# Convolution inputs and gates of the first mixer: from feature-major units to token-major seven-product passes

## The chip, the cores and the metric

The kernel runs on one core of one Trainium2 chip. The metric is the time of one execution on the device, in microseconds (us). PE is TensorE, ACT is ScalarE, DVE is VectorE, SP the queue that issues the DMAs.

## The reference

Two transformer-like blocks run over 256 tokens of width 2048, in float32. The change touches the first mixer of the first block:

```python
proj = h @ w_in        # q, k, v, g_out, gk_low, gate_b, gate_c, xc, merge_a, merge_b
o   = rmsnorm(gla_chunked(q, k, v, log_g))          # 4 heads of 512 value columns
y_a = o * silu(g_out)
y_b = gate_b * causal_depthwise_conv(gate_c * xc, conv_w)    # 3 taps
merged = sigmoid(merge_a) * y_a + sigmoid(merge_b) * y_b
out = merged @ w_out
```

The four projections `gate_c`, `xc`, `gate_b` and `merge_b` (2048 columns each, contraction over 2048) are what is recomputed in another form.

## The kernel before

Every float32 product is made of three products of rounded parts: a weight block W of 128x2048 is read from `raw` (four buffers, filled by SP), ACT rounds it into `w_hi` (L852, "high split"), DVE makes `w_lo` = W - `w_hi` (L1459, "low split"), and PE multiplies `w_hi` with both parts of x, then `w_lo` with the high part. `w_hi` and `w_lo` have two buffers each, so the high split of block n+2 waits until PE has ended the high part of block n, and its low split until PE has ended the low part of block n.

There are two ways to use a block. A *unit* (`unit`, L2540 and L2548) takes 128 output columns over the whole contraction and leaves them with features on partitions. A *pass* (`value_pass`, L2598 to L2623) takes 1024 output columns with tokens on partitions; for the first half of the contraction it makes seven block products where eight were needed (Strassen's scheme in a form due to Winograd: blocks of sums of weights and of x). A pass has 11 forms, each one block:

```python
GATE_1, GM_1, GM_5, GATE_2, GM_6, GM_3, GM_2, GM_7, UP_1, GM_4, UP_2 = range(GATE_FORMS)
```

Four of them (`GATE_1`, `GATE_2`, `UP_1`, `UP_2`) are long: 16 matmuls of `w_hi`, 8 of `w_lo`. The seven GM forms are short: 8 and 4. For four of the short ones DVE first makes a weight sum (`weight_sum`, 128x2048, L1604). ACT copies partial results out of PSUM in the middle of the pass (the state copies), and DVE adds the rest: two sums in the form `UP_1`, two at the start of the next pass.

Before, the stage order of the first mixer is: q and k as units; the values v in two passes; then the convolution stage, a loop over four heads; then `g_out` and `merge_a` in four passes, one for each head (the output passes); then `w_out`. One turn of the convolution loop is 16 units: for each of four tiles of 128 channels the units of `gate_c`, `xc`, `gate_b`, `merge_b`. Between them stand the steps of one head of the linear attention: PE makes the scores (L2874) ahead of unit 0 and the product with the values (L2882) ahead of unit 4; DVE masks the scores (L1684), makes their low part `sc_lo` (L1686) and the inputs of the next head (`stage`, L1556 to L1565); ACT squares the output (L963), takes a root (L966) and scales (L971). The convolution itself is done on DVE tile by tile (L1708 to L1728).

No scheduler is at work: each engine's program is written by hand in the order in which it runs, and semaphores join them. So an instruction that waits holds all that stand behind it on its engine.

## Time and profile before

| what | us |
|---|---|
| median of 3 runs | 2605.47 (2604.85 to 2606.33) |
| profiled execution: its own time | 2606.42 |
| profiled execution: its span | 2604.6 |
| PE busy | 2590.4 |
| DVE busy | 2083.6 |
| ACT busy | 1402.2 |
| conv stage on PE, first scores to first output pass | 190.76 to 564.20 |

The profile is of one execution. Busy time is the time in which an engine has at least one instruction under way. PE's rows overlap: a matmul of 128x512 is shown as some 390 ns long, while the next starts about 227 ns after it, so distances between starts, not durations, tell what PE's work takes.

### The profile page before, as it was taken

What the parts mean: (1) busy time and instruction counts of PE and PEld (TensorE: products, weight loads), DVE (VectorE), ACT (ScalarE), POOL (GpSimd) and SP (SyncE); (2) the same over time, 40 slices, a digit from 0 to 9 for tenths busy, and PEclk for the clock granted to TensorE, in tenths of its full rate; (3) what the DMA queues carried; (4) which work ended last, traced back from release to release, by engine and by line L of the source; (5) the groups of instructions that cost most, each with busy time, mean ns of one, the idle gap of its engine ahead of it and who ended that gap; (6) DMA issues with size and microseconds to landing.
All of it is one profiled execution on the core that took longest, in us unless ns stands there. A gap on an engine that the chain in (4) does not pass through costs nothing.

```text
span 2604.6 us, 34491 instructions
## 1 busy us (share of the span) xinstructions
PE 2590.4 (99%) x13138; PEld 2208.1 (85%) x13138; DVE 2083.6 (80%) x1902; ACT 1402.2 (54%) x1331; POOL 3.5 (0%) x8
## 2 busy tenths in 40 slices
PE   9999999999999999999999999999999999999998
PEld 8888888888888888888888888888888888888887
DVE  7886666679967999879998878897777787677888
ACT  6554444456756565546565556536554455444454
POOL 0000000000000000000000000000000000000000
PEclk9999999999999999999999999999999999999999
DMA  6464454546564646555655554534455545555554
GB/s 246 175 226 176 178 184 176 184 170 222 180 243 176 226 177 225 184 207 179 225 182 210 190 218 162 176 143 178 162 181 190 184 170 210 206 183 191 187 220 142
DMA packets 71892, 497.52 MB, mean 191 GB/s; under 512 B 8183, under 2 KB 9432, under 8 KB 12648
## 3 DMA queue, kind: packets, MB, share of 16 engines
q1 hardware_dynamic: 71784, 496.06, 52.6%
q8 instruction: 70, 1.15, 0.2%
q14 instruction: 38, 0.31, 0.0%
HBM read 493.93 MB, written 2.10 MB: 190 GB/s over the span
## 4 chain that ended last, share of the span: by engine, by line
PE 95%; DVE 2%; ACT 1%; DMA 1%; issue 0%; SPq 0%; DVEq 0%; ACTq 0%
PE acc L2540 27%; PE acc L2598 20%; PE acc L2548 14%; PE acc L2605 10%; PE acc L2623 6%; PE acc L2617 5%; PE acc L2619 5%; PE acc L2734 1%; DVE w_lo L1459 1%; ACT w_hi L852 1%; PE acc L2958 1%; DMA mask_s<-in_mask 1%; PE acc L2742 1%; PE aux L3040 1%; PE aux L3099 1%; DMA raw<-in_w_down 0%
## 5 line engine op out<-in xcount | busy, mean ns | idle before, releaser
L852 ACT ACTIVATE w_hi<-raw 128x2048 fp32r<-128x2048 f32 (+1 forms) x483 | 921.3, 1909 | 723.3 <-PE acc L2540 265.7
L1459 DVE TENSOR_TENSOR w_lo<-raw,w_hi 128x2048 fp32r<-128x2048 f32 (+1 forms) x483 | 1099.8, 2280 | 188.9 <-ACT w_hi L852 178.2
L2540 PE MATMUL acc<-xa,w_hi 128*128 128x512 f32 x3104 | 743.0, 391 | 0.0
L2540 PEld LDWEIGHTS acc<-xa,w_hi 128*128 128x128 f32 x3104 | 571.4, 188 | 112.3 <-issue 0.7
L2548 PEld LDWEIGHTS acc<-xa,w_lo 128*128 128x128 f32 x3104 | 397.9, 191 | 15.0
L2548 PE MATMUL acc<-xa,w_lo 128*128 128x256 f32 x3104 | 402.9, 283 | 0.0
L2598 PE MATMUL acc<-w_hi,xa 128*128 128x512 f32 x1152 | 273.2, 389 | 0.0
L2598 PEld LDWEIGHTS acc<-w_hi,xa 128*128 128x128 f32 x1152 | 215.9, 188 | 44.8
L2598 PE MATMUL acc<-w_hi,hid 128*128 128x512 f32 x768 | 183.3, 390 | 1.4 <-ACT w_hi L852 1.4
L1471 DVE TENSOR_TENSOR tmp<-acc,small 128x512 f32<-128x512 f32 x76 | 52.5, 691 | 150.7 <-ACT small L862 150.4
L2598 PEld LDWEIGHTS acc<-w_hi,hid 128*128 128x128 f32 x768 | 143.5, 188 | 32.0 <-ACT w_hi L852 2.2
L2605 PE MATMUL acc<-w_lo,xa 128*128 128x512 f32 x576 | 142.3, 389 | 0.0
L2605 PEld LDWEIGHTS acc<-w_lo,xa 128*128 128x128 f32 x576 | 108.1, 188 | 22.5
L852 ACT ACTIVATE w_hi<-w_sum 128x2048 fp32r<-128x2048 f32 x36 | 69.1, 1920 | 69.8 <-PE acc L2598 20.2
L1459 DVE TENSOR_TENSOR w_lo<-w_sum,w_hi 128x2048 fp32r<-128x2048 f32 x36 | 82.4, 2290 | 26.5 <-ACT w_hi L852 26.4
L1377 ACT ACTIVATE tmp<-tmp 128x256 f32<-128x256 f32 x44 | 18.4, 418 | 151.9 <-DVE tmp L2406 151.9
L2605 PE MATMUL acc<-w_lo,hid 128*128 128x512 f32 x384 | 95.2, 389 | 0.0
L2605 PEld LDWEIGHTS acc<-w_lo,hid 128*128 128x128 f32 x384 | 72.0, 188 | 15.0
L2617 PE MATMUL acc<-w_hi,xa 128*128 128x512 f32 x192 | 74.8, 390 | 0.0
L2619 PE MATMUL acc<-w_hi,xa 128*128 128x512 f32 x192 | 74.7, 389 | 0.0
L2617 PE MATMUL acc<-w_hi,g_hi 128*128 128x512 f32 x160 | 63.1, 395 | 0.0
L2619 PE MATMUL acc<-w_hi,g_lo 128*128 128x512 f32 x160 | 62.3, 390 | 0.0
(423 smaller groups left out, 2954.5 us busy)
## 6 DMA issues: line engine op xcount, KB each, us to landing
raw<-in_w_in SPq DMA_DIRECT2D x158, 1024.0 KB, 4.8
raw<-in_w_gate_up SPq DMA_DIRECT2D x88, 1024.0 KB, 4.8
raw<-in_w_down SPq DMA_DIRECT2D x88, 1024.0 KB, 4.8
raw<-in_w_up SPq DMA_DIRECT2D x87, 1024.0 KB, 4.8
raw<-in_w_out SPq DMA_DIRECT2D x32, 1024.0 KB, 4.8
raw<-in_w_uq SPq DMA_DIRECT2D x3, 1024.0 KB, 4.9
h_tok<-in_x_tok SPq DMA_DIRECT2D x1, 2048.0 KB, 10.7
raw<-in_w_ukv SPq DMA_DIRECT2D x4, 512.0 KB, 3.2
```

What stands on the lines that cost most here:

```text
L852: act.activation(hi_part(u, run)[:, 0:kt * P], raw_of(u)[:, 0:kt * P], ACT.Copy).then_inc(hi_made, splits(u, run))
L1459: dve.tensor_tensor(lo_part(u, run)[:, 0:kt * P], raw_of(u)[:, 0:kt * P], hi_part(u, run)[:, 0:kt * P], ALU.subtract).then_inc(lo_made, sp ...
L1471: dve.tensor_tensor(tmp[:, 0:2], acc[:, b:b + 2, 0:S], small[:], ALU.add).then_inc(acc_free, 2)
L2540: last = pe.matmul(acc[:, bnk], w_hi[:, u % SPLIT, k * P:(k + 1) * P], x[:, k0 + k], start=first and k == 0, stop=False)
L2548: last = pe.matmul(acc[:, bnk, S:2 * S], w_lo[:, u % SPLIT, k * P:(k + 1) * P], x[:, k0 + k, 0:S], start=False, stop=final and k == kt - 1)
L2598: last = pe.matmul(acc[:, bank(t + c)], a, w, start=(first and k == 0 and half == 0), stop=False, skip_group_check=more)
L2605: last = pe.matmul(acc[:, bank(t + c)], x[:, k0 + k, c * P:(c + 1) * P], lo_part(u, 0)[:, k * 512:(k + 1) * 512], start=False, stop=(final ...
L2617: pe.matmul(acc[:, bank(t)], x_hi(k), w, start=(first and k == 0), stop=False, skip_group_check=more)
L2619: last = pe.matmul(acc[:, bank(t)], x_lo(k), w, start=False, stop=False, skip_group_check=more)
L2623: last = pe.matmul(acc[:, bank(t)], x_hi(k), w_lo[:, u % SPLIT, k * 512:(k + 1) * 512], start=False, stop=(final and k == 3), skip_group_c ...
L2734: last = pe.matmul(acc[:, bank(tiles[c])], x[:, tile, half * S + c * P:half * S + (c + 1) * P], w_hi[:, u % SPLIT, k * 512:(k + 1) * 512], ...
L2742: last = pe.matmul(acc[:, bank(tiles[c])], x[:, tile, c * P:(c + 1) * P], w_lo[:, u % SPLIT, k * 512:(k + 1) * 512], start=False, stop=fin ...
```

## The change

The 64 units of the convolution stage become 8 passes (11 blocks each, 88 in all), two for each head: the first computes `gate_c` and `xc`, the second `merge_b` and `gate_b`. The results now have tokens on partitions and stand in `halves`. DVE multiplies the two of a pass with each other and with the row scale; PE transposes the product (8 transposes, `turn_product`) behind the form `GM_1` of the next pass; ACT makes the middle tap and DVE the two outer taps from the transposed tiles; the gate product is transposed too and multiplied in by `gated_conv_out`. The head's steps are put into the first pass of each pair: PE's scores behind `GATE_1`, the values behind `GM_2`. The high part of v is now made on ACT. The loop over heads is written out. In the second block's FFN, the first split of each first down pass is made a little earlier and one state copy is put behind a split. Here is the core of the diff:

On ACT:

```diff
+            def value_high(hd):
+                act.wait_ge(acc_free, T_V + 4 * (hd // 2) + 8)
+                act.activation(v_hi[:], v_tok[:, hd], ACT.Copy).then_inc(o_parts_made, 1)
+            def middle_taps(hd):
+                for t in range(4):
+                    i = 4 * hd + t
+                    act.activation(yb[:, i], aux[:, t // 2, t % 2 * S:(t % 2 + 1) * S], ACT.Copy,
+                                   scale=column("conv_w", i + 2 * DT)).then_inc(conv_mid, 1)
+            def conv_gate(hd):
+                for c in range(2):
+                    act.wait_ge(acc_free, T_CONV + 8 * hd + 4 + c + 5)
+                    act.activation(halves[:, c], halves[:, c], ACT.Sigmoid, scale=rstd_t[:, c:c + 1]).then_inc(gate_out, 2)
...
+            for k, u in enumerate(CONV_STARTS):
+                hd, second = k // 2, k % 2
+                for form in range(GATE_FORMS):
+                    if form == GM_7:
+                        conv_state(k, GM_7, 3, 1)
+                    split(u + form + 2)
+                    if form == GM_1 and not second:
+                        value_high(hd)
+                    if form == GM_5:
+                        if k:
+                            act.wait_ge(turned, k + 1)
+                        conv_state(k, GM_1, 3, 0)
+                    if form == GATE_2:
+                        conv_state(k, GM_5, 2, 3)
+                    if form == GM_6:
+                        conv_state(k, GM_6, 3, 2)
+                        if second:
+                            middle_taps(hd)
+                        else:
+                            act.wait_ge(masked, hd + 1)
+                            act.activation(sc_hi[:], sc[:], ACT.Copy).then_inc(sc_hi_made, 1)
+                    if form == GM_2:
+                        prepare(ACT.Sigmoid if second else ACT.Sqrt)
+                    if form == GM_7 and not second:
+                        act.wait_ge(o_made, hd + 1)
+                        for c in range(2):
+                            act.activation(o_n[:, c], aux[:, c], ACT.Square, accum_out=o_sum[:, c:c + 1]).then_inc(o_squared, 1)
+                    if form == UP_1 and not second:
+                        act.wait_ge(var_made, hd + 2)
+                        act.activation(o_var[:], o_var[:], ACT.Sqrt).then_inc(std_made, 1)
+                    if form == GM_4 and not second:
+                        act.wait_ge(o_scale, hd + 1)
+                        for c in range(2):
+                            act.activation(v_tok[:, hd, c], aux[:, c], ACT.Copy, scale=o_rstd[:, c:c + 1]).then_inc(o_read, 1)
+                if second:
+                    conv_gate(hd)
```

On DVE:

```diff
+            def conv_sum(k, form, tile, n, state):
+                u = CONV_STARTS[k]
+                dve.wait_ge(lo_used, u + form + 1)
+                dve.wait_ge(snapped, sums_before(u) + state)
+                dve.tensor_tensor(halves[:, n], halves[:, n], acc[:, bank(T_CONV + 4 * k + tile)], ALU.add).then_inc(acc_free, 1)
...
+            def conv_product(k):
+                conv_sum(k, UP_2, 2, 2, 3)
+                conv_sum(k, UP_2, 3, 3, 2)
+                dve.wait_ge(acc_free, T_CONV + 4 * k + 8)
+                if k % 2:
+                    dve.wait_ge(gate_out, 2 * k + 4)
+                for c in range(2):
+                    dve.scalar_tensor_tensor(halves[:, c], halves[:, 2 + c], (rstd_t if k % 2 else rstd_2)[:, c:c + 1], halves[:, c],
+                                             ALU.mult, ALU.mult).then_inc(gate_in, 1)
...
+            def outer_taps(hd):
+                for back in (1, 2):
+                    for t in range(4):
+                        i = 4 * hd + t
+                        if back == 1:
+                            dve.wait_ge(conv_mid, i + 1)
+                        elif t == 0:
+                            step.wait()
+                        tail = yb[:, i, back:S]
+                        step(dve.scalar_tensor_tensor(tail, aux[:, t // 2, t % 2 * S:(t % 2 + 1) * S - back],
+                                                      column("conv_w", i + (2 - back) * DT), tail, ALU.mult, ALU.add))
+            def gated_conv_out(hd):
+                dve.wait_ge(turned, 2 * hd + 3)
+                step.wait()
+                y = yb[:, 4 * hd:4 * hd + 4]
+                dve.tensor_tensor(y, y, aux[:, 2:4].rearrange("p b (a s) -> p (b a) s", s=S), ALU.mult).then_inc(op_f32, 4)
...
+            for k, u in enumerate(CONV_STARTS):
+                hd, second = k // 2, k % 2
+                if k:
+                    conv_product(k - 1)
+                for form in range(GATE_FORMS):
+                    split(u + form + 2)
+                    if form == GATE_1:
+                        weight_sum(u, 2)
+                    if form == GM_5:
+                        weight_sum(u, 3)
+                        if not second:
+                            value_low(hd)
+                    if form == GATE_2 and not second:
+                        dve.wait_ge(scores_made, hd + 1)
+                        dve.tensor_tensor(sc[:], aux[:, 0, 0:3 * P], mask_s[:], ALU.mult).then_inc(masked, 1)
+                    if form == GM_3:
+                        weight_sum(u, 4)
+                        if not second:
+                            dve.wait_ge(sc_hi_made, hd + 1)
+                            dve.tensor_tensor(sc_lo[:], sc[:], sc_hi[:], ALU.subtract).then_inc(o_parts_made, 1)
+                    if form == GM_7:
+                        if second:
+                            outer_taps(hd)
+                        else:
+                            if hd:
+                                gated_conv_out(hd - 1)
+                            if hd + 1 < HEADS:
+                                stage(hd + 1)
+                    if form == UP_1:
+                        conv_sum(k, GM_2, 0, 0, 1)
+                        conv_sum(k, GM_4, 1, 1, 4)
+                        if not second:
+                            dve.wait_ge(o_squared, 2 * hd + 2)
+                            dve.tensor_scalar(o_var[:], o_sum[:], 1.0 / DV, EPS, ALU.mult, ALU.add).then_inc(var_made, 1)
+                    if form == GM_4:
+                        if not second:
+                            dve.wait_ge(std_made, hd + 2)
+                            dve.reciprocal(o_rstd[:], o_var[:]).then_inc(o_scale, 1)
+                        weight_sum(u + GATE_FORMS, 1)
+            conv_product(2 * HEADS - 1)
```

On PE (`scores` and `head_values` are the matmuls of L2874 and L2882 behind their new waits):

```diff
                 by_tokens(u + GATE_1, b_11, xa, 8, 4, True, False)
+                if scores:
+                    scores()
...
                 product(u + GM_2, b_11, *block_of(xa, 4, 0), final=True)
+                if values:
+                    values()
...
+            def scores(hd):
+                pe.wait_ge(staged, hd + 1)
+                pe.wait_ge(gate_in, 4 * hd + 2)
...
+            def head_values(hd):
+                pe.wait_ge(o_parts_made, 3 * hd + 3)
...
+            def turn_product(k):
+                pe.wait_ge(gate_in, 2 * k + 4)
+                pe.wait_ge(*((op_f32, 4 * (k // 2)) if k % 2 else (o_read, k + 2)))
+                for m in range(4):
+                    for c in range(2):
+                        at_ = m % 2 * S + c * P
+                        last = pe.transpose(aux[:, k % 2 * 2 + m // 2, at_:at_ + P], halves[:, c, m * P:(m + 1) * P], ident[:])
+                last.then_inc(turned, 1)
...
+            for k, u in enumerate(CONV_STARTS):
+                value_pass(u, T_CONV + 4 * k, (lambda: turn_product(k - 1)) if k else None,
+                           *(((lambda: scores(k // 2)), (lambda: head_values(k // 2))) if k % 2 == 0 else ()))
```

In the second FFN, on ACT and DVE (the down passes' first splits):

```diff
+                        if g == 0 and form == M_7:
+                            first_out(u, t, 3, M_7, 2 * p, 1)
+                        if p or form != PLAIN_1:
+                            split(u + form + 2)
                         if g == 0 and form == M_6:
...
+                        if last and p:
+                            weight_sum(u0 + 2 * GT, 1)
+                            split(u0 + 2 * GT + M_1)
```

The order of the instructions on two engines shows where the head's steps now stand. First DVE, in the middle of the first pass of head 1 (L1459 before and L1492 now are the low split, L1604 and L1636 the weight sum). Before, one turn of the loop has, between two of the head's splits:

```order
L1714 SCALAR_TENSOR_TENSOR qkv<-tmp,vec,qkv 128x254
L1683 REGISTER_ALU
L1684 TENSOR_TENSOR sc<-aux,mask_s 128x384
L1686 TENSOR_TENSOR sc_lo<-sc,sc_hi 128x384
L1456 REGISTER_ALU
L1459 TENSOR_TENSOR w_lo<-raw,w_hi 128x2048
```

And now:

```order
L1764 TENSOR_TENSOR sc<-aux,mask_s 128x384
L1492 TENSOR_TENSOR w_lo<-raw,w_hi 128x2048 x2
L1636 TENSOR_TENSOR raw<-raw,v_sum 128x2048
L1769 TENSOR_TENSOR sc_lo<-sc,sc_hi 128x384
L1492 TENSOR_TENSOR w_lo<-raw,w_hi 128x2048 x2
L1748 TENSOR_TENSOR qkv<-qkv,aux 128x1024
```

The low part of the scores has moved from right behind the mask to behind two splits and a weight sum.

Second ACT, around the root of the head's variance (L852 before and L854 now are the high split, L963/L1006 the squares, L971/L1013 the scaled copies). Before:

```order
L862 ACTIVATE small<-acc 128x512
L965 REGISTER_ALU
L966 ACT_TABLE_LOAD
L966 ACTIVATE o_var<-o_var 128x2
L849 REGISTER_ALU
L852 ACTIVATE w_hi<-raw 128x2048
```

And now, from the squares on:

```order
L854 ACTIVATE w_hi<-raw 128x2048
L1006 ACTIVATE o_n,o_sum<-aux 128x512 x2
L854 ACTIVATE w_hi<-raw 128x2048
L1009 ACTIVATE o_var<-o_var 128x2
L854 ACTIVATE w_hi<-raw 128x2048
L1013 ACTIVATE v_tok<-aux,o_rstd 128x512 x2
L854 ACTIVATE w_hi<-raw 128x2048
L854 ACTIVATE w_hi<-v_sum 128x2048
L854 ACTIVATE w_hi<-raw 128x2048
```

The root and the copies now stand directly between the high splits of the last forms of the pass and of the first forms of the next one.

## Rows read from the trace of the kernel before

**Rows 1.** Page, parts 1 and 4: busy time by engine, chain that ended last.
```profile
PE 2590.4 (99%) x13138; PEld 2208.1 (85%) x13138; DVE 2083.6 (80%) x1902; ACT 1402.2 (54%) x1331; POOL 3.5 (0%) x8
...
PE 95%; DVE 2%; ACT 1%; DMA 1%; issue 0%; SPq 0%; DVEq 0%; ACTq 0%
```

**Rows 2.** Waits of PE over the span (us in total, times, longest).
```profile
PE acc L2598 <- ACT w_hi L852: 1.4, 2, 0.8
```

**Rows 3.** Windows, us, then busy PE, PEld, DVE, ACT, POOL; PEclk: three stretches.
```profile
149.96:190.76 40.80, 40.80 (x181) 33.78 (x180) 34.53 (x19) 23.41 (x16) 0.00 (x0) 1.00 0.56 205
...
286.30:379.60 93.30, 93.30 (x543) 82.58 (x542) 62.54 (x72) 42.28 (x38) 0.00 (x0) 1.00 0.50 180
...
605.02:646.73 41.71, 41.71 (x189) 34.61 (x188) 39.54 (x27) 29.42 (x25) 0.00 (x0) 1.00 0.54 199
```

**Rows 4.** Timeline of PE: two units of the convolution's input, by rows of weights.
```profile
222.88 3.82 PE L2540 MATMUL acc<-xa,w_hi 128*128 128x512 f32 x16
...
228.45 3.82 PE L2540 MATMUL acc<-xa,w_hi 128*128 128x512 f32 x16
```

**Rows 5.** Timeline of PE in the third output pass.
```profile
673.94 1.07 PE L2623 MATMUL acc<-w_lo,v_hi 128*128 128x512 f32 x4
674.85 3.79 PE L2598 MATMUL acc<-w_hi,xa 128*128 128x512 f32 x16
...
696.64 1.04 PE L2901 MATMUL aux<-ident,v_tok 128*128 128x128 f32 x8
```

**Rows 6.** Timeline of ACT in the same pass.
```profile
667.86 0.58 ACT L997 ACTIVATE m_tok<-acc 128x512 f32<-128x512 f32 x1
668.75 1.92 ACT L852 ACTIVATE w_hi<-raw 128x2048 fp32r<-128x2048 f32 x1 [0.32 <-PE acc L2619]
...
675.54 1.91 ACT L852 ACTIVATE w_hi<-raw 128x2048 fp32r<-128x2048 f32 x1
```

**Rows 7.** Timeline of DVE in the same pass.
```profile
670.71 2.29 DVE L1459 TENSOR_TENSOR w_lo<-raw,w_hi 128x2048 fp32r<-128x2048 f32 x1 [0.43 <-ACT w_hi L852]
672.92 2.28 DVE L1604 TENSOR_TENSOR raw<-raw,out_sum_w 128x2048 f32<-128x2048 f32 x1
675.12 4.66 DVE L1459 TENSOR_TENSOR w_lo<-raw,w_hi 128x2048 fp32r<-128x2048 f32 x2
679.69 1.65 DVE L1742 SCALAR_TENSOR_TENSOR qkv<-aux,vec,qkv 128x256 f32<-128x256 f32 x4
681.27 2.28 DVE L1459 TENSOR_TENSOR w_lo<-raw,w_hi 128x2048 fp32r<-128x2048 f32 x1
683.47 1.28 DVE L1756 TENSOR_TENSOR g_tok<-g_tok,acc 128x512 f32<-128x512 f32 x2
684.66 1.22 DVE L1749 TENSOR_TENSOR xb<-qkv,xb 128x1024 fp32r<-128x1024 f32 x1
```

**Rows 8.** Timelines of ACT and DVE: four scaled copies; two 512-column products.
```profile
770.36 1.55 ACT L1029 ACTIVATE xa<-aux,vec 128x256 fp32r<-128x256 f32 x4
...
152.56 1.40 DVE L1647 SCALAR_TENSOR_TENSOR v_tok<-acc,rstd_t,v_tok 128x512 f32<-128x512 f32 x2
```

**Rows 9.** Groups by line in the conv stage: the head's small operations.
```profile
L971 ACT ACTIVATE v_tok<-aux,o_rstd 128x512 f32 x8 | 5.0, 675 | 0.0
...
L1686 DVE TENSOR_TENSOR sc_lo<-sc,sc_hi 128x384 fp32r<-128x384 f32 x4 | 2.2, 558 | 2.4 <-ACT sc_hi L959 2.4
...
L966 ACT ACTIVATE o_var<-o_var 128x2 f32<-128x2 f32 x4 | 0.8, 204 | 0.0
```

**Rows 10.** Timeline of DVE: first of the nine of `stage`, and the split behind them.
```profile
235.96 0.16 DVE L1556 COPY dec<-e_b 128x8 f32 x1
...
239.03 2.29 DVE L1459 TENSOR_TENSOR w_lo<-raw,w_hi 128x2048 fp32r<-128x2048 f32 x1 [0.30 <-DVE q_far L1565]
```

**Rows 11.** Windows at the end of the program, columns as in rows 3.
```profile
2590.00:2597.00 7.00, 6.22 (x28) 4.81 (x26) 5.20 (x11) 1.04 (x4) 0.00 (x0) 1.00 0.33 112
2597.00:2600.00 3.00, 0.00 (x0) 0.00 (x0) 2.90 (x7) 0.99 (x3) 0.00 (x0) 0.85 0.20 77
```

More of the change, by code:

```diff
@@ L1377, in gated @@
                         act.activation(tmp[:, 2], tmp[:, 2], ACT.Gelu_apprx_tanh).then_inc(gate_out, 1)
[L1378 removed]
+                        if not (ahead == 2 and p == 0):
                             split(u + 4, run)
@@ L2391, in _, with gated @@
                 v0, g0 = V_FF2 + g * GT, G_FF2 + g * GT
-                def gated(run, pairs, ahead=0, between=None):
+                def gated(run, pairs, ahead=0, between=None, last=False):
                     for p in range(2):
```

211 lines of the change are left out of this document (62 added, 149 removed).

## The prediction

> **What bounds the kernel now.** I read the page first: PE is busy for 99% of the span and makes 95% of the chain that ended last [rows 1]. In the list of PE's waits the first entry is 1.4 us, in two waits of at most 0.8, at the start of the second FFN's down passes [rows 2]. So the kernel is PE's own work, back to back, and a change pays by what it takes off PE, less what it makes PE wait. The windows by stage then tell how near the others are: in a value pass DVE is busy for 34.5 of 40.8 us, in a head of the convolution stage for 62.5 of 93.3, in an output pass, which also has transposes and merges, for 39.5 of 41.7 [rows 3]. The new passes are of that last kind and carry more, so the timelines of PE, ACT and DVE in one output pass are what the rest is worked out from [rows 5 to 7].
>
> **PE's own work.** A unit takes 5.57 us from start to start [rows 4], eight of them 44.5; a pass for the same 1024 columns takes 40.8 [rows 3]. Eight passes save 8 x 3.73 = 29.8 us. Each pass's product is turned by 8 transposes: the output pass with transposes is 41.71, the one without 40.80, so 0.91 each, 8 x 0.91 = 7.3 us back. Scores and values are the same matmuls as before. PE's work alone: -22.5 us. In the down passes the earlier split can give back up to the 1.4 us of [rows 2]; I take -1.4, the other end is 0.
>
> DVE's work grows too: 11 low splits and 4 weight sums a pass, 2.2 us each from start to start [rows 7], are 33 us; four sums 2.4, two products 1.4 [rows 8]. With the head's steps the first pass of a pair comes to some 43 of PE's 45.9 us, the second to some 40 of 41.7. On the average this fits. But a pass has fixed meeting points, and the sum of busy times does not show them. I walk through them in order of time, against T, PE's end of the form `GM_7` (674.85 in [rows 5]). From T, PE has `UP_1` 5.44, `GM_4` 2.72, `UP_2` 5.44 and the next `GATE_1` 5.44: it wants `GATE_1` at T+13.6 and `GM_1` at T+19.1 (the transposes behind `GM_1` start at 696.64, less 2.72).
>
> **Wait 1, values for the low scores, four times.** In the output pass PE starts the low part of `GM_7` at 673.94, so `GM_7` itself began, and `GM_2` ended, at 672.13. DVE's weight sum 4 began at 672.92 and its next instruction at 675.12, 3.0 us behind `GM_2` [rows 5, 7]. It can't be earlier: its split of `GM_7` waits for ACT's high split, which ACT starts when PE has ended the high part of `GM_3` (668.75, idle 0.32 before it [rows 6]). In the first pass of a head `sc_lo` stands behind this weight sum, 0.56 us [rows 9], and PE's values stand ahead of `GM_7`. With a hop of 0.1 between engines and 0.1 for the high part of the scores on ACT, PE waits 3.8 us: 15.2 us. That DVE doesn't take `sc_lo` sooner is in its order: the pair of splits at 675.12 starts right behind the weight sum [rows 7]. The Trainium skill (TensorE: Matmul & The Clock Gate, Architectural detail) says that ACT and DVE are strict FIFO; this trace agrees. Were it otherwise, `sc_lo` could go ahead of the weight sum, the wait would be 1.6 us, and the sum below would be 8.8 us lower.
>
> **Wait 2, `GATE_1` of the second pass, heads 1 and 2.** DVE has ended the splits behind T at T+4.84 (679.69). Now follow `gated_conv_out` 1.1 (1024 columns, half of a split's 2.2), `stage` 3.07 [rows 10], a split 2.2, two sums 1.2 (busy 1.28, [rows 7]), the variance 0.2: T+12.6. ACT's root, 0.20 [rows 9], stands ahead of the high split of the next `GATE_1`, 1.92: ready at T+14.9, against 13.6. 1.3 us for heads 1 and 2, 0.15 for head 0 (no product of a head before it), none for head 3 (no `stage`): 2.8 us.
>
> **Wait 3, `GM_1` of the second pass, four times.** From that high split on: low split 2.3, reciprocal 0.2, ACT's two scaled copies 1.3 [rows 9], the high split of `GM_1` 1.9, its low split 2.2, the two sums 1.2 that free PE's last bank, hops: 9.2 us, while PE has 5.44 of `GATE_1`. 3.8 us for heads 0 to 2. For head 3 DVE is 3.1 us earlier and PE waits from T+19.1 to T+21.3: 2.2. Together 13.6 us.
>
> **Wait 4, scores for the product, three times.** In the second pass ACT makes four middle taps (1.55 us, [rows 8]) between its state copy at 667.86 and the high split at 668.75. That split, and DVE's chain behind it, come 1.1 us later; the low part of `GM_7` waits 0.2 (four times, 0.8 us), and DVE ends the two splits at T+5.8. Then eight taps 3.35 (two groups like L1742's, 1.58 each, and a drain), split 2.2, sums 1.2, split, weight sum, split 6.6, sums 1.2: T+20.3; the two products 1.4 and hops: T+21.9. PE's scores stand at T+19.1 and wait for it: 2.8 us for heads 1 to 3, 8.4 us. Ahead of the first output pass `GM_1` waits for the sums alone: 1.3.
>
> **The sum.** -29.8 + 7.3 + 15.2 + 2.8 + 13.6 + 0.8 + 8.4 + 1.3 - 1.4 = +18.2 us. On the profiled execution's own 2606.4 that is 2624.6; the median of the runs is 0.9 below that execution, so **2623.7 us**, slower by 0.7%. What I cost at nothing: the DMAs (as many blocks of the same size as before, and the same freeing order as in the output passes, where PE doesn't wait for them), the high part of v on ACT (half of a high split's 1.92 us, in a form in which ACT has time: it is busy for 29 of 41.7 us [rows 3]), and the written-out loop. Were this cover gone, each late load would be one more wait of PE's. Bounds: the gate product and the taps, which read PSUM, may take what a 512-column pair takes in [rows 8] (0.3 us more each); each of the 18 waits may be 0.3 us off either way. That gives 2617 to 2631 for this case.
>
> **Rivals.** (a) *PE never waits.* DVE's total fits, and the sum of PE's work alone decides: 2606.4 - 22.5 - 1.4, median 2581.6, faster. It needs DVE to run ahead of PE, which the double buffers of `w_hi` and `w_lo` forbid: in [rows 7] DVE itself idles 0.43 us for ACT's high split. Chance 0.04. (b) *Only wait 1 is real.* At the pass ends DVE catches up, because taps, `stage` and the small steps overlap better than start-to-start distances say. The point is the sums' end, T+19.1; if they are there, waits 2 to 4 are nothing: 2606.4 - 22.5 - 1.4 + 15.2, median 2596.8, faster by 0.3%. For it: an output pass with 39.5 us of DVE's work doesn't wait at all. Against it: that pass has no `stage`, and no root between two high splits. Chance 0.09. (c) *Half of waits 2 to 4*, median 2610, chance 0.05. (d) *The clock falls in the long waits.* PE's last matmul ends at 2596.2 (6.22 us busy of the first 7), and in the next window the granted clock is 0.85 as a mean, so it fell from the upper level (2.4 GHz) to the lower (1.2 GHz) about 3 us after PE went idle [rows 11]. Waits 1 and 3 are 3.8 us, seven in all. If each is followed by as long a stretch at half speed, each costs 1.9 us more, 13 us: median 2637. The page named above (Part 1) holds that an idle array goes to the lower clock and that sustained work brings it back; the rows show the first. How soon it comes back no row shows; the waits of [rows 2] are too short to tell. Chance 0.12.
>
> **How the numbers follow.** Forecast 0.70, (a) 0.04, (b) 0.09, (c) 0.05, (d) 0.12. The range runs from 2609, which leaves out (a), (b) and a part of (c), to 2635, which leaves out the far half of (d). A measurement of this kernel tells a change of 0.2%, 5.2 us, from none. Faster by more than that: (a) and (b), 0.12. Within it, up to 2610.7: half of (c) and a little of the forecast, 0.06. Slower: 0.82.
>
> **What would show it.** In the changed profile PE should wait, in the list of waits, for `sc_lo` four times by 3.8 us, for the sums of `halves` in the second passes by 3.8, for the products ahead of the scores by 2.8, and for ACT's high split once or twice by 1.3. Passes should last about 50, 46, 52, 47, 52, 47, 52 and 44 us, the stage from the first scores on some 20 us longer than the 373 of before. If the first pass of a head lasts 46 us, wait 1 is wrong; if the second lasts 42, waits 2 and 3 are. A granted clock below 1.00 inside the stage speaks for (d).

## The result and the profile after

| what | before | after |
|---|---|---|
| median of 4 runs, us | 2605.9 (2604.85 to 2606.44) | 2633.1 (2629.8 to 2633.92) |
| ratio | | 1.0103 [1.009, 1.0115] |
| profiled execution: its own time | 2606.42 | 2629.8 |
| profiled execution: its span | 2604.6 | 2627.9 |
| conv stage on PE, to the first output pass | 373.4 | 398.1 |
| mean granted clock of the profiled execution | 0.999 | 0.995 |

The changed kernel is slower by 27.2 us, 1.0%. The forecast was 2623.7, in a range of 2609 to 2635. The later part of the program, from the end of the first output pass (605.02 before, 630.66 now) to the end of the span, is 2.3 us shorter, so the loss lies ahead of it: the convolution stage is 24.7 us longer and the first output pass 1.9 us, while the stage starts 1.0 us earlier (189.76 for 190.76), by shorter waits at the program's start.

The page of the changed kernel, parts 1 and 4, beside [rows 1]:

```profile
PE 2581.5 (98%) x12594; PEld 2176.6 (83%) x12594; DVE 2168.5 (83%) x1879; ACT 1452.3 (55%) x1373; POOL 3.5 (0%) x8
...
PE 91%; DVE 5%; issue 2%; ACT 1%; DMA 0%; DVEq 0%; SPq 0%; ACTq 0%
```

PE has 544 matmuls less, and is still only 8.9 us less busy; the windows below show why. The waits of PE over the span (us in total, times, longest), beside [rows 2]:

```profile
PE aux L2947 <- DVE sc_lo L1769: 13.7, 4, 3.4
PE acc L2679 <- DVE halves L1712: 11.9, 5, 3.3
PE aux L2938 <- DVE halves L1722: 7.0, 3, 2.4
PE acc L2660 <- ACT w_hi L854: 1.9, 2, 0.9
```

These are the four waits of the forecast, with its counts: the values for `sc_lo`, `GM_1` for the sums (four second passes and the first output pass), the scores for the product, `GATE_1` behind the root. A matmul row is 0.39 us long where the next would start after 0.23, so each idle time is shown 0.16 us too short. The timeline of DVE in the first pass of head 0 shows how the first of them comes about:

```profile
212.45 2.28 DVE L1492 TENSOR_TENSOR w_lo<-raw,w_hi 128x2048 fp32r<-128x2048 f32 x1
215.09 2.29 DVE L1492 TENSOR_TENSOR w_lo<-raw,w_hi 128x2048 fp32r<-128x2048 f32 x1 [0.36 <-ACT w_hi L854]
217.30 2.28 DVE L1636 TENSOR_TENSOR raw<-raw,v_sum 128x2048 f32<-128x2048 f32 x1
219.50 0.55 DVE L1769 TENSOR_TENSOR sc_lo<-sc,sc_hi 128x384 fp32r<-128x384 f32 x1
```

And PE in the same stretch:

```profile
215.61 1.07 PE L2685 MATMUL acc<-w_lo,xa 128*128 128x512 f32 x4
220.11 0.60 PE L2947 MATMUL aux<-v_hi,sc_hi 128*128 128x512 f32 x1 [3.43 <-DVE sc_lo L1769]
220.50 0.63 PE L2947 MATMUL aux<-v_hi,sc_lo 128*128 128x512 f32 x1
220.93 0.63 PE L2947 MATMUL aux<-v_lo,sc_hi 128*128 128x512 f32 x1
...
223.86 0.40 PE L2679 MATMUL acc<-w_hi,v_hi 128*128 128x512 f32 x1
224.09 0.39 PE L2681 MATMUL acc<-w_hi,v_lo 128*128 128x512 f32 x1
```

`GM_2` ends at 216.52 (four matmuls from 215.61). DVE is then 0.8 us away from a weight sum of 2.2 us, and only behind it stands the small operation that PE waits for. Between the matmuls of the values, the rows show a second thing: behind the wait the matmuls start 0.43 us apart, until 223.86, and 0.23 us apart from there on. The windows at six places (us, busy PE, PEld, DVE, ACT, POOL, then PEclk) show the same:

```profile
220.00:224.00 4.00, 3.89 (x10) 3.11 (x11) 2.25 (x2) 0.00 (x0) 0.00 (x0) 0.57 0.59 201
295.00:299.00 4.00, 4.00 (x17) 3.48 (x16) 3.07 (x2) 0.00 (x0) 0.00 (x0) 0.57 0.04 14
350.00:354.00 4.00, 4.00 (x12) 3.09 (x12) 3.96 (x4) 0.66 (x1) 0.00 (x0) 0.57 0.56 233
397.50:401.50 4.00, 4.00 (x17) 3.37 (x16) 2.78 (x2) 0.00 (x0) 0.00 (x0) 0.57 0.00 0
452.00:456.00 4.00, 4.00 (x11) 3.15 (x12) 3.96 (x4) 0.59 (x1) 0.00 (x0) 0.57 0.64 248
500.00:504.00 4.00, 4.00 (x15) 3.27 (x14) 2.49 (x2) 0.00 (x0) 0.00 (x0) 0.57 0.00 0
```

In most of each window the clock stood at its lower level (1.2 for 2.4 GHz): 0.43 x 4 = 1.7 us of work lost, 10.2 us in six. I call one such stretch a fall. Everywhere else in the stage the granted clock is 1.00. (In the experiments the falls are counted in the same way, from the granted clock in windows of half a microsecond; a stretch twice as long, with 3.4 us lost, counts as two falls in a row.) PE's busy time counts a slow matmul as busy, so these 10.2 us stand under PE's work, and that is the main reason why its busy time has gone down so little.

The end of a first pass, where the second and the third wait are made, in the timeline of ACT (head 1):

```profile
329.96 1.93 ACT L854 ACTIVATE w_hi<-raw 128x2048 fp32r<-128x2048 f32 x1
338.64 0.20 ACT L1009 ACTIVATE o_var<-o_var 128x2 f32<-128x2 f32 x1 [6.75 <-DVE o_var L1783]
338.75 1.90 ACT L854 ACTIVATE w_hi<-raw 128x2048 fp32r<-128x2048 f32 x1
343.08 1.27 ACT L1013 ACTIVATE v_tok<-aux,o_rstd 128x512 f32<-128x512 f32 x2 [2.44 <-DVE o_rstd L1787]
344.24 1.92 ACT L854 ACTIVATE w_hi<-raw 128x2048 fp32r<-128x2048 f32 x1
```

ACT stands still for 6.75 us, until DVE has made the variance, ahead of a root of 0.20 us, and the high split that PE needs for `GATE_1` (340.79, idle 0.94) stands behind it; then for 2.44 us ahead of the copies, with the high split of `GM_1` behind them (PE: 349.73, idle 3.25).

### The profile page after: what moved, and what is told of

The parts are those of the page before. It is cut to its first block, busy times and chain, and to the rows that moved or that the text cites. A ratio compares the mean times of both kernels' runs of the same rounds, so it can differ in the third digit from the quotient of the medians.

```text
span 2627.9 us, 32728 instructions
## 1 busy us (share of the span) xinstructions
PE 2581.5 (98%) x12594; PEld 2176.6 (83%) x12594; DVE 2168.5 (83%) x1879; ACT 1452.3 (55%) x1373; POOL 3.5 (0%) x8
## 4 chain that ended last, share of the span: by engine, by line
PE 91%; DVE 5%; issue 2%; ACT 1%; DMA 0%; DVEq 0%; SPq 0%; ACTq 0%
PE acc L2660 22%; PE acc L2602 18%; PE acc L2667 11%; PE acc L2610 9%; PE acc L2679 7%; PE acc L2685 7%; PE acc L2681 7%; DVE w_lo L1492 2%; PE acc L2800 1%; ACT w_hi L854 1%; DVE halves L1712 1%; DVE raw L1636 1%; PE acc L3030 1%; PE acc L2808 1%; PE aux L3112 1%
## 5 line engine op out<-in xcount | busy, mean ns | idle before, releaser
L854 ACT ACTIVATE w_hi<-raw 128x2048 fp32r<-128x2048 f32 (+1 forms) x491 | 936.9, 1909 | 666.7 <-PE acc L2660 203.1
L1492 DVE TENSOR_TENSOR w_lo<-raw,w_hi 128x2048 fp32r<-128x2048 f32 (+1 forms) x491 | 1117.9, 2280 | 219.7 <-ACT w_hi L854 212.0
L2602 PE MATMUL acc<-xa,w_hi 128*128 128x512 f32 x2080 | 498.4, 392 | 0.0
L2602 PEld LDWEIGHTS acc<-xa,w_hi 128*128 128x128 f32 x2080 | 383.0, 188 | 75.6 <-issue 0.7
L2660 PE MATMUL acc<-w_hi,xa 128*128 128x512 f32 x1664 | 394.8, 389 | 1.9 <-ACT w_hi L854 1.9
L2660 PEld LDWEIGHTS acc<-w_hi,xa 128*128 128x128 f32 x1664 | 311.9, 188 | 67.6 <-issue 2.9
L2610 PEld LDWEIGHTS acc<-xa,w_lo 128*128 128x128 f32 x2080 | 266.6, 191 | 10.0
L2610 PE MATMUL acc<-xa,w_lo 128*128 128x256 f32 x2080 | 270.1, 283 | 0.0
L2667 PE MATMUL acc<-w_lo,xa 128*128 128x512 f32 x832 | 205.5, 389 | 0.0
L2667 PEld LDWEIGHTS acc<-w_lo,xa 128*128 128x128 f32 x832 | 156.1, 188 | 32.5
L2679 PE MATMUL acc<-w_hi,xa 128*128 128x512 f32 x288 | 117.2, 407 | 11.9 <-DVE halves L1712 11.9
L2681 PE MATMUL acc<-w_hi,xa 128*128 128x512 f32 x288 | 115.9, 402 | 0.0
L854 ACT ACTIVATE w_hi<-w_sum 128x2048 fp32r<-128x2048 f32 x36 | 69.1, 1919 | 71.7 <-PE acc L2660 20.2
L1492 DVE TENSOR_TENSOR w_lo<-w_sum,w_hi 128x2048 fp32r<-128x2048 f32 x36 | 82.4, 2290 | 30.3 <-ACT w_hi L854 30.2
L2679 PE MATMUL acc<-w_hi,v_hi 128*128 128x512 f32 x224 | 88.2, 394 | 0.0
L2681 PE MATMUL acc<-w_hi,v_lo 128*128 128x512 f32 x224 | 87.2, 389 | 0.0
L2667 PEld LDWEIGHTS acc<-w_lo,hid 128*128 128x128 f32 x384 | 72.1, 188 | 14.9
```

The lines of the kernel that those rows point to most:

```text
L854: act.activation(hi_part(u, run)[:, 0:kt * P], raw_of(u)[:, 0:kt * P], ACT.Copy).then_inc(hi_made, splits(u, run))
L1492: dve.tensor_tensor(lo_part(u, run)[:, 0:kt * P], raw_of(u)[:, 0:kt * P], hi_part(u, run)[:, 0:kt * P], ALU.subtract).then_inc(lo_made, sp ...
L2602: last = pe.matmul(acc[:, bnk], w_hi[:, u % SPLIT, k * P:(k + 1) * P], x[:, k0 + k], start=first and k == 0, stop=False)
L2610: last = pe.matmul(acc[:, bnk, S:2 * S], w_lo[:, u % SPLIT, k * P:(k + 1) * P], x[:, k0 + k, 0:S], start=False, stop=final and k == kt - 1)
L2660: last = pe.matmul(acc[:, bank(t + c)], a, w, start=(first and k == 0 and half == 0), stop=False, skip_group_check=more)
L2667: last = pe.matmul(acc[:, bank(t + c)], x[:, k0 + k, c * P:(c + 1) * P], lo_part(u, 0)[:, k * 512:(k + 1) * 512], start=False, stop=(final ...
```

## The experiments

The theory is that each wait is made at one meeting point, by the place in which a small step stands on DVE or ACT, and that falls of the clock come on top of it (M). Its rivals are that DVE's total work sets the length of the passes, so that a wait taken away comes back at the next point (L), and that the clock has nothing to do with the waits. Each time is the median of five executions (e6 four, e10 six, e8 eleven); the changed kernel is the base of every edit but the last one's, e8. Its median of 2633.1 us is that of the result above and was not taken again beside the edits, where the kernel before gave 2605.2 to 2605.9. Since its profiled execution is 3.3 us below its median, a difference of medians is often larger than one of profiled spans; sizes of waits and falls are compared with the spans.

### The low part of the scores

**e1: `sc_lo` ahead of weight sum 4.**

```diff
                     if form == GM_3:
+                        if not second:
+                            dve.wait_ge(sc_hi_made, hd + 1)
+                            dve.tensor_tensor(sc_lo[:], sc[:], sc_hi[:], ALU.subtract).then_inc(o_parts_made, 1)
                         weight_sum(u, 4)
-                        if not second:
-                            dve.wait_ge(sc_hi_made, hd + 1)
-                            dve.tensor_tensor(sc_lo[:], sc[:], sc_hi[:], ALU.subtract).then_inc(o_parts_made, 1)
```

> Edit: on DVE, in the first pass of each head, the low part of the scores (sc_lo) stands ahead of weight sum 4 instead of behind it. Theory M (meeting points): PE's wait ahead of the values is set by DVE's order. The weight sum is 2.2 us from start to start, so the wait falls from 3.4 us to about 1.2 in each of the four heads, 8.8 us in all, and the stretch at the lower clock behind it (220.11 to 223.86 in the changed kernel, 3.75 us at half speed, 1.9 us lost) goes as well, since the wait is then as short as those behind which the clock stays: 8.8 + 7.5, from 2633.1 to about 2617. Theory L (load): the pair of passes is as long as DVE's work lets it be. Then what is taken from this wait comes back at GM_1 of the second pass, and the time stays within 3 us of 2633.

Measured: 2621.1 us, 12.0 less. In the waits of PE:

```profile
PE acc L2679 <- DVE halves L1712: 11.9, 5, 3.2
PE aux L2938 <- DVE halves L1722: 7.0, 3, 2.4
PE aux L2947 <- DVE sc_lo L1768: 4.9, 4, 1.2
```

The wait is 1.2 us, and the other waits are as they were: M's size, and nothing comes back. The profiled spans differ by 8.6 us (2627.9 and 2619.3), the 8.8 us of the waits. The expectation had also counted four falls of the clock that would go, and that was misread: in the changed kernel only the first of the four waits for `sc_lo` has one behind it, and this kernel too has six, all at the other waits and four of them as two pairs. The first pair begins while PE still stands, which starts `GM_1` only at 442.73 (columns as above, the clock third from the end):

```profile
442.00:442.50 0.50, 0.00 (x0) 0.00 (x0) 0.50 (x2) 0.00 (x0) 0.00 (x0) 0.50 0.21 82
...
447.50:448.00 0.50, 0.50 (x2) 0.22 (x1) 0.50 (x1) 0.50 (x1) 0.00 (x0) 0.50 0.00 0
```

**e2: both parts of the scores earlier.** ACT's high part in `GATE_2`, DVE's low part behind its split in `GM_6`.

```diff
                     if form == GATE_2:
                         conv_state(k, GM_5, 2, 3)
+                        if not second:
+                            act.wait_ge(masked, hd + 1)
+                            act.activation(sc_hi[:], sc[:], ACT.Copy).then_inc(sc_hi_made, 1)
...
+                    if form == GM_6 and not second:
+                        dve.wait_ge(sc_hi_made, hd + 1)
+                        dve.tensor_tensor(sc_lo[:], sc[:], sc_hi[:], ALU.subtract).then_inc(o_parts_made, 1)
```

> Edit: ACT makes the high part of the scores in the form GATE_2, right behind the mask, and DVE the low part behind its split in GM_6, one form and a weight sum earlier than before. Theory M: the wait for sc_lo (13.7 us in four) is gone, and so are the four stretches at the lower clock behind it (1.9 us each): 13.7 + 7.5, from 2633.1 to about 2612. Theory L: DVE's load sets the length of the pair of passes; the waits for the sums of halves and for the products grow by what is taken here, and the time stays above 2625.

Measured: 2620.4 us. The wait for `sc_lo` is gone, but a new one stands in the list, and that for low splits is 0.9 us longer than it was:

```profile
PE acc L2679 <- ACT w_hi L854: 3.9, 4, 1.0
...
PE acc L2685 <- DVE w_lo L1492: 1.5, 6, 0.5
```

ACT's timeline names their maker:

```profile
212.63 0.53 ACT L996 ACTIVATE sc_hi<-sc 128x384 fp32r<-128x384 f32 x1 [3.37 <-DVE sc L1764]
213.06 1.90 ACT L854 ACTIVATE w_hi<-raw 128x2048 fp32r<-128x2048 f32 x1
```

ACT is early, holds 3.37 us for DVE's mask, and the high split of `GM_2` behind it is late. So a third of the gain (3.9 + 0.9 of 13.7 us) was given back, as this reads, by a hold on another engine and not by DVE's load. The next run tells whether that reading is right.

**e10: only DVE's `sc_lo` moved**, with the last three lines of the diff above and ACT as in the changed kernel.

> Edit: DVE's sc_lo alone moves, from behind weight sum 4 to behind the low split that DVE makes in the form GM_6; ACT's order stays as in the changed kernel. The run with both moved (2620.4 us) turned 13.7 us of waiting for sc_lo into 3.9 us for ACT's high split and 0.9 more for low splits. If that came from ACT's high part of the scores standing too early (ACT holds for DVE's mask, and the next high split behind it is late), it is gone here: no wait for sc_lo, and none in its place, 14 us off 2633.1, so 2617 to 2619, with as many falls of the clock as the other waits make (five or six, 1.7 us each). If sc_lo in that place delays DVE's own later splits instead, PE waits for w_lo or w_hi by 1 us a head as before and the time stays at 2620 to 2622.

Measured: 2613.7 us, 19.4 less than the changed kernel and 3.3 below the expected 2617 to 2619. No wait for `sc_lo` is left and none for ACT's high split in its place. DVE:

```profile
212.32 2.28 DVE L1492 TENSOR_TENSOR w_lo<-raw,w_hi 128x2048 fp32r<-128x2048 f32 x1
214.52 0.55 DVE L1767 TENSOR_TENSOR sc_lo<-sc,sc_hi 128x384 fp32r<-128x384 f32 x1
214.99 2.29 DVE L1492 TENSOR_TENSOR w_lo<-raw,w_hi 128x2048 fp32r<-128x2048 f32 x1
217.19 2.29 DVE L1636 TENSOR_TENSOR raw<-raw,v_sum 128x2048 f32<-128x2048 f32 x1
```

The operation of 0.5 us fits into the place where DVE idled 0.36 us for ACT in the changed kernel; the splits behind it are not later. One moved instruction, four times in the program, gives back 19.4 of the 27.2 us that were lost. By the profiled spans it is 16.5 us: 13.7 of idle time, 4 x 0.16 that the rows hide, and one fall less (five in place of six).

### The end of the first pass

**e3: variance, root, reciprocal and copies one to two forms earlier.**

```diff
 # DVE, form GM_7 of the first pass
+                            dve.wait_ge(o_squared, 2 * hd + 2)
+                            dve.tensor_scalar(o_var[:], o_sum[:], 1.0 / DV, EPS, ALU.mult, ALU.add).then_inc(var_made, 1)
                             if hd:
                                 gated_conv_out(hd - 1)
                             if hd + 1 < HEADS:
                                 stage(hd + 1)
+                            dve.wait_ge(std_made, hd + 2)
+                            dve.reciprocal(o_rstd[:], o_var[:]).then_inc(o_scale, 1)
 # ACT: the root right behind the squares, the copies in UP_1 for GM_4
```

> Edit: in the first pass of a head the variance stands behind DVE's splits of GM_7, ACT's root right behind its squares, the reciprocal behind stage, and ACT's two scaled copies in the form UP_1: the chain variance, root, reciprocal, copies ends one to two forms earlier. Theory M: wait 2 (GATE_1 of the second pass, 1.9 us in two) goes, and wait 3 (GM_1 of the second pass, 11.1 us in four) shrinks to 0.4 us in head 0 and about 1.5 in heads 1 and 2, where gated_conv_out and stage still stand ahead of the sums: 8 to 10 us less, and two or three of the six falls of the clock (1.7 us each) with it, so 2618 to 2623. Rival: the sums come late by DVE's own work (stage, gated_conv_out, splits), not by the root; then GM_1 waits as before, only wait 2 changes, and the time is 2630 or more.

Measured: 2622.0 us, 11.1 less. The wait at `GATE_1` is gone, and the one at `GM_1`:

```profile
PE acc L2676 <- DVE halves L1711: 3.2, 3, 1.2
```

1.2 us in heads 1 and 2, none in heads 0 and 3, and 0.8 at the first output pass. M, by its sizes. The spans differ by 9.3 us; the idle times fell by 10.6, four waits that are gone had 0.16 more each, and one fall of 1.7 came to it (seven).

**e4: e3, and `stage` spread over the first half.**

```diff
                     if form == GATE_1:
                         weight_sum(u, 2)
+                        if not second and hd + 1 < HEADS:
+                            dve.wait_ge(scores_made, hd + 1)
+                            stage(hd + 1, 0)
+                    if form == GM_1 and not second and hd + 1 < HEADS:
+                        stage(hd + 1, 1)
+                    if form == GM_2 and not second and hd:
+                        gated_conv_out(hd - 1)
```

> Edit: as in e3_root_early, and in addition stage is cut in two and stands in the forms GATE_1 and GM_1 of the first pass, gated_conv_out in GM_2. Theory M: waits 2 and 3 (1.9 + 11.1 us) are gone and with them the falls of the clock behind GM_1: 13 + 2 to 3 x 1.7 off 2633.1, so 2615 to 2618. Rival (load in the first half): DVE must now wait for the scores before it makes the next head's inputs and carries 3.1 us more work ahead of the mask; then sc_lo comes later and wait 1 grows from 3.4 us by 1 to 3 us in heads 0 to 2, and 3 to 9 us are given back: 2619 to 2627.

Measured: 2618.0 us median, the profiled execution 2623.2. The waits at `GATE_1` and at `GM_1` of the second passes are gone; the wait for `sc_lo` grew from 13.7 to 14.2 in all (3.9 in head 0), so the rival is worth 0.5 us of its 3 to 9. What kept the profiled execution up is the clock: ten falls, 17 us. Its five runs go from 2615.4 at a granted clock of 0.996 to 2623.9 at 0.992.

### The taps

**e5: middle taps in `GM_5`, outer taps in `GATE_2` and `GM_6` of the second pass.**

```diff
+                    if form == GATE_2 and second:
+                        outer_taps(hd, (1,))
+                    if form == GM_6 and second:
+                        outer_taps(hd, (2,))
                     if form == GM_7:
-                        if second:
-                            outer_taps(hd)
 # ACT: middle_taps(hd) in GM_5 for GM_6
```

> Edit: in the second pass of a head ACT's middle taps stand in GM_5 instead of GM_6, and DVE's outer taps in GATE_2 (four) and GM_6 (four) instead of all eight in GM_7. Theory M: the sums and products at the end of the second pass are 3.4 us earlier against PE, and the wait for the products ahead of the scores (7.0 us in three) and the one ahead of the first output pass are gone: 7 to 8 us, and the three falls of the clock behind them (1.7 us each), so 2621 to 2626. Rival: DVE is late in the first half of the second pass (wait 3 stands there), so the taps delay its splits and PE waits for w_lo or w_hi in GM_6 to GM_7 by what was gained: 2630 or more.

Measured: 2622.6 us, 10.5 less. The wait ahead of the scores is gone (7.0 us in three). The last line answers to the rival:

```profile
PE acc L2681 <- DVE halves L1712: 11.1, 4, 3.2
PE acc L2662 <- ACT w_hi L854: 1.9, 2, 1.0
PE acc L2687 <- DVE w_lo L1492: 1.7, 5, 0.5
```

Low splits are late by 1.1 us more in all than in the changed kernel (0.6), so a seventh of the gain is given back; the first output pass waits no more (11.1 for 11.9). Four falls are left of six.

### The clock

**e6: matmuls that nothing reads, ahead of the values' wait.**

```diff
             def head_values(hd):

+                for _ in range(16):
+                    pe.matmul(aux[:, 1], xa[:, 0, 0:P], xa[:, 0], start=True, stop=True)
                 pe.wait_ge(o_parts_made, 3 * hd + 3)
```

> Edit: 16 matmuls of 128x512 that nothing reads stand ahead of PE's wait for sc_lo, four times; at 0.227 us each they are 3.6 us, about as long as the wait. Nothing else is changed. If the clock falls because PE stands still there, the values and GM_7 then run at the upper level and the time falls by 4 x 1.9 = 7.5 us, to about 2626. If the fall has another cause, or the slow rows are only how the trace shows them, the time stays at 2633 or rises by the part of the 16 that the wait does not cover (0.2 us each, below 1 us).

Measured: 2630.1 us, 3.0 less, in a spread of the runs of 3 us; the profiled spans are 2628.4 and 2627.9, the same. Two windows of this kernel:

```profile
220.50:224.00 3.50, 3.50 (x17) 2.89 (x16) 2.11 (x1) 0.00 (x0) 0.00 (x0) 1.00 0.56 190
247.50:251.50 4.00, 3.62 (x9) 2.91 (x10) 3.94 (x4) 0.00 (x0) 0.00 (x0) 0.57 0.74 262
```

The values now run at full speed, but `GM_1` behind the next wait does not, where in the changed kernel it did. Six falls as before: one has moved. The expected 7.5 us failed for the reason named at e1.

**e9: the same ahead of all long waits.**

```diff
+            def filled(hd, n):
+                pe.wait_ge(op_f32, 4 * hd)
+                for _ in range(n):
+                    pe.matmul(aux[:, 2], xa[:, 0, 0:P], xa[:, 0], start=True, stop=True)
...
 # ahead of the scores of heads 1 to 3: filled(hd - 1, 11)
 # ahead of the wait of GM_1, second passes: filled(k // 2, 7 if k == 7 else 15)
```

> Edit: as in the kernel before this one, and in addition 11 such matmuls ahead of the scores of heads 1 to 3 (wait 2.4 us) and 15 ahead of GM_1 of the second pass of heads 0 to 2 (wait 3.3 us), 7 in the last head. If all the stretches at the lower clock come from PE's standing still, the granted clock is 1.00 in the whole stage and the time falls by the four behind sc_lo (7.5 us) and the six others (2.6 us or less at half speed, some 1 us lost each): 13 us, to about 2620. What is left above the kernel before is then the waits alone. If the waits behind which the stretches are shorter cost nothing in clock, it is no faster than the one before it, 2626.

Measured: 2620.8 us, 12.3 less (9.2 by the profiled spans, against 10.2 for six falls), with the same waits for the same semaphores in the program; PE now works while it would stand. The runs lie within 2.0 us of each other. The stage:

```profile
190.00:600.00 410.00, 407.30 (x1856) 335.20 (x1855) 348.97 (x260) 232.23 (x206) 0.00 (x0) 1.00 0.49 172
```

1.00 where the changed kernel has 0.98, and no fall. A kernel with 149 useless matmuls (64 + 33 + 52) and every semaphore in place is 12 us faster, so the falls are a cost of their own, and where PE does not stand still for long there are none.

**e13: all but the values' waits filled** (e9 without the lines of e6).

> Edit: the counterpart of e6_values_filled: the filling matmuls stand ahead of the scores and of GM_1 of the second passes as in e9_all_filled, and not ahead of the values, so only the four waits for sc_lo (3.4 us) are left standing. In the changed kernel one of its six falls of the clock (1.7 us each) came in the first wait for sc_lo, and filling those waits alone left six. If a wait of 3.4 us gives a fall by itself, four falls are left, 6.8 us above the 2620.8 of e9_all_filled: 2627 to 2628. If a fall comes only now and then from it, as the three unslowed waits for sc_lo in the changed kernel say, one or two are left and the time is 2622 to 2624. If the waits for sc_lo give no fall of themselves, the time is that of e9_all_filled.

Measured: 2625.8 us, 5.0 above e9; the profiled span is 5.1 above e9's. It has three falls of 1.7 us, two in a row at the second wait for `sc_lo` and one at the third, none at the first and the last, though all four waits are 3.4 us in the rows. The three lie between the expectation's four and its one or two. So such a wait gives falls by itself, but not each time, and one wait can give two.

### Together

**e11: e10 + e4 + e5.** **e12: e10 + e3 + e5**, with `stage` left where it was.

> Edit: the moves of e10_low_behind_split, e4_stage_spread and e5_taps_early together; the matmuls of the changed kernel are all there. Theory M: each wait was made at a meeting point by the order in which small steps stand on DVE and ACT, so with all of them moved PE runs back to back, 22.5 us below the kernel before, less the 2.3 us that the end of the program has gained, plus what the single runs left (1.1 us more for w_lo, 0.8 for the first output pass): 2605.4 - 22.5 - 2.3 + 2, so 2581 to 2585, with no fall of the clock in the stage. Theory L (DVE's load): the waits went one at a time because the others gave DVE time to catch up. With none left a pair of passes has 87.6 us of PE and some 83 of DVE's busy time, and waits for w_lo, for sc_lo or for the sums come up again by 1 to 3 us a head: 2588 to 2600.

> Edit: as in e11_all_moves, but stage and gated_conv_out stay where the changed kernel has them, in GM_7 of the first pass (the moves of e10, e3 and e5). Theory M: what is left against e11_all_moves is the wait at GM_1 of the second pass in heads 1 and 2, 1.2 us each, 2.4 us in all: 2583 to 2588, and no fall of the clock, since waits of 1.2 us had none behind them in e3_root_early. Theory L: DVE's splits come late at several places and it is 5 us or more above e11_all_moves, or equal to it if spreading stage over the first half costs as much as it gives.

Measured: e11 2584.8 us, ratio to the kernel before 0.9919 [0.9906, 0.9933]; e12 2587.9, ratio 0.9933 [0.992, 0.9947]. Both beat both kernels. e11's longest waits of PE, the first of them at the start of the program and two of the other four in the stage:

```profile
PE acc L2902 <- ACT w_hi L890: 1.7, 1, 1.7
PE acc L2690 <- DVE w_lo L1491: 1.4, 4, 0.5
```

and its stage, from `GATE_1` of the first pass to the first output pass:

```profile
190.84:544.05 353.21, 351.98 (x1614) 291.14 (x1613) 330.29 (x249) 220.48 (x195) 0.00 (x0) 1.00 0.54 191
```

DVE is busy for 330.3 of 353.2 us, 94%, and PE's waits in the stage are 1.0 us in the rows, in three: L has fallen. Of e12's waits 2.4 us stand at `GM_1`, as expected, and its median is 3.1 above e11.

**e8: the kernel before with the FFN edit alone** (the lines on the second FFN of the diff and no others).

> Edit: the kernel before with the edit in the second FFN alone (the first split of each first down pass earlier, one state copy behind a split); the convolution stage is that of before. PE waited there 0.78 and 0.62 us for w_hi, and 0.2 twice for w_lo: 1.4 to 1.8 us off the 2605.4 of before, so 2603.6 to 2604.0. If the 2.3 us by which the later part of the changed kernel is shorter all come from this edit, 2603.1. If PE only waits elsewhere for what is moved, 2605.4.

Measured: 2604.0 us against 2605.75, ratio 0.9992 [0.9983, 1.0001], and the wait of [rows 2], 1.4 us, is out of its list; one wait for a low split has grown from 0.2 to 0.5 us. That would leave some 1.4 us, with 0.16 added to each of the two waits that are gone. The interval of the ratio just takes in no change.

## Why the prediction was right, and where it was not

| term, us | forecast | profile after |
|---|---|---|
| PE's own work, eight passes with transposes | -22.5 | -20.8 |
| wait 1, values for `sc_lo` | 15.2 | 14.4 |
| wait 2, `GATE_1` behind the root | 2.8 | 2.2 |
| wait 3, `GM_1` for the sums | 13.6 | 11.8 |
| low part of `GM_7` | 0.8 | 0 |
| wait 4, scores for the product | 8.4 | 7.5 |
| first output pass | 1.3 | 0.9 |
| second FFN (measured: all behind the first output pass) | -1.4 | -2.3 |
| waits at the program's start | 0 | -1.0 |
| falls of the clock | 0 | 10.2 |
| sum | +18.2 | +22.9 |

The right column has the idle times of the rows with 0.16 us added to each; the profiled execution itself is 23.4 us above that of before. PE's own work is read from e11: 353.2 less 373.4 is -20.2, less 1.0 us of idle time left in its stage and 0.5 that the rows hide; that stage has seven of the eight sets of transposes, and the eighth makes e11's first output pass 0.9 us longer than before (41.7 for 40.8).

**PE's own work** gave 1.7 us less than the forecast, and e11 shows that the 20.8 us are there to be had. Where the 1.7 us went is not shown; a wait below 0.16 us stands in no row, and the written-out loop, which was put at nothing, can cost no more than that. **Waits 1 to 4** were right in place, engine, count and order: the head without `stage` waits less at `GM_1` (1.5 against 3.2), head 0 does not wait at `GATE_1`, head 0 has no product to wait for. Each is 0.2 to 0.6 us shorter than worked out, 5.3 us in all with the low part of `GM_7`, which didn't wait, and the first output pass. (For head 3 at `GM_1` the forecast's own chain gives 1.9 us, not 2.2: T+14.9 less 3.1 plus 9.2 is T+21.0.) The one case that can be read to the end is wait 1: from `GM_2`'s end the sum starts after 0.78 (forecast 0.79) and `sc_lo` after 2.98, and PE starts 0.06 after its end; the 0.2 us put down for a hop and for ACT's high part weren't there, since that part had been made long before. The experiments remove each wait by its own small move, e10 the first, e3 the second and most of the third, e4 both, e5 the fourth, and the others stay as they are.

**The step that failed is the clock, which the sum has at nothing.** The forecast took the waits at their bare length and gave 0.12 to rival (d), that the clock falls in them; it did, for 10.2 us in the profiled execution. It said that waits 1 and 3, seven in all, are each followed by a stretch at half speed that costs 1.9 us, 13 us. The runs show six falls of 1.7 us in the profiled execution, by the waits ahead of the scores too, which (d) had left out (2.5 us long), and neither behind three of the four waits for `sc_lo` nor behind `GM_1` in head 0. The total of (d) was near, the list of places was not. The forecast gave its own case 2617 to 2631 us, and 2633.1 lies outside that; it lies in the stated range because that left room for a part of (d). And that it is not further off is in part luck: waits worked out 5.3 us too long make up for half of the falls. With the measured terms, the sum for the median would have been 2623.7 - 5.3 + 1.7 - 0.9 - 1.0 + 10.2 = 2628.4; the remaining 4.7 us are mainly the difference between the profiled execution, the fastest of the four, and the other three, which have granted clocks of 0.993 and 0.994 for its 0.995. Two more falls would make 3.4 us; that is read from the granted clocks only, since just the profiled execution has a trace.

**Rival (a)**, PE never waits, 2581.6: not this kernel, but e11 (2584.8), so what the rival said about DVE's total was true and the fixed order was what stood against it. **Rival (b)**, only wait 1 is real: fallen with the list of waits. (The chances of (a) and (b) add up to 0.13, where the forecast has 0.12.) **Rival (c)**, half of waits 2 to 4: fallen, 22.4 of their 26.9 us came (with the first output pass). **Costs put at nothing**: no wait of the stage names a DMA, and none the high part of v. **Pass lengths**: forecast 50, 46, 52, 47, 52, 47, 52, 44; measured 50.4, 45.6, 55.0, 47.2, 55.0, 47.2, 54.0, 43.8. The third, fifth and seventh are longer than forecast mainly by their fall of 1.7 us, and the third and fifth also hold wait 2, which I had put into the pass behind it.

## What to carry to other kernels

DVE, busy for 83% of the span and 94% of e11's stage, did not bound this kernel, but one small operation behind a long one on it cost 14.4 us. For every operation that another engine waits for, ask what stands directly ahead of it in its queue, and put it behind the piece of work that makes room for it. When a small step is moved forward, look at what the engine that makes its input will hold for (e2 gave back a third that way, e10 did not). And an idle time of TensorE of 2.35 us or more in the rows often cost more than its length here (six falls for ten such waits in the changed kernel). Price such waits as a range, with and without a slow stretch each, since no run shows which of them gets one.

## What the hardware showed that was not expected

- **A fall costs about the same after any wait that has one.** Each one is 1.7 us of lost work, whether the wait was 2.35 us in the rows (scores) or 3.4, less what of it lies in PE's idle time. Its place varies: behind the first scores' wait of the changed kernel PE starts at 293.72 and the windows are at the lower level from 295.0 on; in e1's pair at 442 the clock had fallen before PE started.
- **Equal waits, unequal falls.** Four waits of 3.4 us for `sc_lo` had one fall in the changed kernel, four in e3, and falls at two of four in e13, one of them a pair. The ten falls of e4 go with 7 long waits, the four of e5 with 7, the six of e1 with 6. No wait of 1.2 us had one (e1, e3, e12). The Trainium skill (TensorE: Matmul & The Clock Gate, Part 1) says that the chip's look at TensorE's activity is free-running and not tied to the kernel; that fits waits that are sometimes hit and sometimes not, but no run here was made to test it.
- **A pair of falls goes with an early one.** In all eight pairs (three in e4, two in e1, one each in e2, e5 and e13; read in windows of 0.1 us) the clock had fallen 0.4 us or more before PE started again: in e4 at 291.6 with the start at 292.03, in e5 at 415.3 with 416.65. Of the 36 single falls, two began more than 0.1 us ahead of PE's start (e10 at 340.1 with 340.56, e13 at 420.5 with 420.81). So the order goes together with the double cost in these traces; what decides it stays open.
- **It spreads the times.** The kernels with long waits differ from run to run by up to 8.5 us (e4) and follow the granted clock (e5: 2619.6 at 0.997, 2625.4 at 0.994), those without, and the filled one, by 0.9 to 2.3 us at 0.999 (e9, e11, e12).
- **The useful part of filling.** 149 useless matmuls in the time of the waits gave 12.3 us. It is a way to price the clock; taking the waits away (e11) gave 48.3.
